# A hybrid mixer block: pacing the weight block sums and moving second-layer modulation products

## The reference

```python
mod = split(silu(c) @ ada_w[l] + ada_b[l], 6)             # for the latents
mod_c = split(silu(c_ctx) @ ada_w[l] + ada_b[l], 6)       # for the context
h = modulate(rmsnorm(x, norm1_w[l]), mod[0], mod[1])
p = split_cols(h @ w_in[l])                               # A, B, C, D and the gates
x = x + mod[2] * gated_merge([ya, yb, yg, yd], p[4], w_branch[l], w_o[l])
x = x + mod[5] * sqrelu_mlp(modulate(rmsnorm(x, norm2_w[l]), mod[3], mod[4]), mlp_w1[l], mlp_w2[l])
```

## Time and profile before

| | us |
|---|---|
| median of 3 runs | 2919.35 (2917.09 to 2925.95) |
| the profiled execution | 2913.71 |
| its span | 2911.9 |
| TensorE busy | 2754.0 |
| VectorE busy | 1728.8 |
| ScalarE busy | 1421.1 |
| GpSimd busy | 212.7 |
| mean granted clock of TensorE | 0.983 |

### The profile page before, as it was taken

One profiled execution on the slowest core, in us unless ns is written; L12 is line 12 of the kernel. 1 busy time (PEld: TensorE's weight loads), 2 busy tenths in 40 slices (PEclk: granted clock), 3 DMA queues, 4 the chain that ended last, 5 costly groups with the idle time before them and its releaser, 6 DMA issues.

```text
span 2911.9 us, 36847 instructions
## 1 busy us (share of the span) xinstructions
PE 2754.0 (95%) x14456; PEld 2299.8 (79%) x14456; DVE 1728.8 (59%) x2539; ACT 1421.1 (49%) x2335; POOL 212.7 (7%) x259
## 2 busy tenths in 40 slices
PE   6999999989989999899899999999999999999998
PEld 4888886778877778788899878777667776788887
DVE  4478843436645546887989552784547644654434
ACT  4644434435635545767676444444546635433222
POOL 0023311011001000000000000321000000000000
PEclk9999999999999999999999999999999999999999
DMA  6322167098269134345566232224021220423232
GB/s 243 116 66 71 64 208 179 15 273 213 77 193 263 41 131 152 125 152 162 185 204 210 82 107 68 88 95 146 11 92 62 88 66 20 165 82 100 94 98 90
DMA packets 100022, 356.46 MB, mean 122 GB/s; under 512 B 11216, under 2 KB 11472, under 8 KB 98640
## 3 DMA queue, kind: packets, MB, share of 16 engines
q1 hardware_dynamic: 79936, 248.19, 25.5%
q0 software_dynamic: 19920, 105.99, 13.2%
HBM read 327.91 MB, written 84.94 MB: 142 GB/s over the span
## 4 chain that ended last, share of the span: by engine, by line
PE 41%; DVE 6%; ACT 3%; issue 2%; DMA 1%; SPq 0%; DVEq 0%; ACTq 0%
PE slot L860 35%; PE slot L1394 4%; DVE wl L2185 1%; PE slot L1361 1%; DVE ada_prod L2844 1%; DMA raw<-w_merge_dram 1%; ACT b_high L2024 1%; ACT ada_prod L1965 1%; DMA raw<-w_dram 0%; ACT wh L1511 0%; DVE b_low L2774 0%; DVE X L2794 0%; ACT UR L2046 0%; DMA SS<-g_kept 0%; PE slot L1071 0%
## 5 line engine op out<-in xcount | busy, mean ns | idle before, releaser
L860 PE MATMUL slot<-Hh,wh 128*128 128x512 f32 (+1 forms) x1872 | 701.3, 376 | 29.5 <-issue 11.8
L860 PE MATMUL slot<-Hh,wl 128*128 128x512 f32 (+1 forms) x1872 | 665.7, 357 | 0.0
L860 PE MATMUL slot<-Hl,wh 128*128 128x512 f32 (+1 forms) x1872 | 664.8, 356 | 0.0
L2185 DVE TENSOR_TENSOR wl<-raw,wh 128x1024 fp32r<-128x1024 f32 (+1 forms) x374 | 430.4, 1151 | 278.8 <-ACT wh L1511 276.2
L1511 ACT ACTIVATE wh<-raw 128x1024 fp32r<-128x1024 f32 (+1 forms) x374 | 366.5, 981 | 390.7 <-PE slot L860 237.8
L860 PEld LDWEIGHTS slot<-Hh,wh 128*128 128x128 f32 x1872 | 357.4, 191 | 85.2 <-issue 25.3
L860 PEld LDWEIGHTS slot<-Hh,wl 128*128 128x128 f32 x1872 | 356.2, 191 | 51.4
L860 PEld LDWEIGHTS slot<-Hl,wh 128*128 128x128 f32 x1872 | 357.9, 192 | 48.0 <-issue 6.0
L1394 PE MATMUL slot<-b_high,wh 128*128 128x384 f32 x784 | 270.3, 345 | 33.1 <-DVE wl L2185 19.6
L1394 PE MATMUL slot<-b_low,wh 128*128 128x384 f32 x784 | 267.1, 341 | 0.0
L1394 PE MATMUL slot<-b_high,wl 128*128 128x384 f32 x784 | 266.8, 340 | 0.0
(11 more groups left out here) (314 smaller groups left out, 4843.5 us busy)
## 6 DMA issues: line engine op xcount, KB each, us to landing
raw<-w_dram SPq DMA_DIRECT2D x190, 512.0 KB, 3.6
raw<-w_gate_dram SPq DMA_DIRECT2D x64, 512.0 KB, 3.5
raw<-w_sums SPq DMA_DIRECT2D x56, 512.0 KB, 3.6
ada_g_raw<-ada_dram POOLq DMA_DIRECT2D x55, 512.0 KB, 4.3
raw<-w_merge_dram SPq DMA_DIRECT2D x64, 256.0 KB, 3.7
w_sums<-w_dram POOLq DMA_DIRECT2D x14, 1024.0 KB, 11.3
w_sums<-w_sums POOLq DMA_DIRECT2D x14, 1024.0 KB, 8.4
ada_g_raw<-ada_dram SPq DMA_DIRECT2D x25, 512.0 KB, 4.5
```

The source lines that it names most:

```text
L860: return pe.matmul(dst, lhsT, rhs, start=start, stop=stop)
L2185: dve.tensor_tensor(wl[to][:, 0:size, :], raw[p][:, 0:size, :], wh[to][:, 0:size, :].bitcast(f32), ALU.subtract).then_inc(low_done.sem, 1)
```

## The change

It changes the order of three kinds of work; what is computed stays the same.

- **Weight block sums.** Phases 0 and 1 go with attention A, 2 and 3 with B, 4 and 5 with D. Before each transfer GpSimd waits (`turn`) until TensorE has done one more attention tile's scores (24 tiles in A and D: one tile a transfer; 48 in B: three tiles a transfer). Phase 6 is issued during the blocks, one transfer after each of 8 modulation tiles.
- **Second layer's one-sided products** (tiles 48 to 79). They leave the blocks for the second layer itself: 10 in C's projection, 8 in D's, 11 in the output product (two each in its jobs 1, 2, 4 and 5), 3 in the first jobs of the MLP. `condition_rows` is issued in the second layer too, before D and before the output product. SyncE loads the tiles. The two-sided tiles 32 to 47 stay in the blocks, now at jobs 29 to 39, 57 to 67 and 85 to 91, every second one. `modulation_ready` for the second norm moves from the first to the last job of the second layer's output product.
- **Four gate tiles** (25 to 28) move from the blocks to the first layer's output product, whose jobs 1, 2, 4 and 5 have two tiles each; the last three stay at block jobs 5, 8 and 11. Of two tiles in a job, VectorE multiplies the first before the split and the second after it.

```diff
-        WEIGHT_SUMS = {"C": (), "A": (0, 1), "B": (2, 3, 4), "D": (5, 6)}
+        WEIGHT_SUMS = {"A": (0, 1), "B": (2, 3), "D": (4, 5)}
...
             if n == FIRST_FF + 1:
-                return 3
+                return 2
...
+        def ada_jobs(layer):
+
+            jobs = list(range(3, 13)) + list(range(FIRST_D[layer], FIRST_D[layer] + KT))
+            for n in range(KT - 1):
+                jobs += [FIRST_FF - KT + n] * (2 if n in (1, 2, 4, 5) else 1)
+            return jobs
+
+        ADA_JOBS = ada_jobs(0)
+        ADA_EARLY, ADA_SECOND, ADA_ALL = len(ADA_JOBS), N_GATE + ADA_BOTH, N_GATE + ADA_TILES
...
+        for t, n in enumerate(ada_jobs(1) + list(range(FIRST_FF + 1, FIRST_FF + 1 + N_GATE - ADA_EARLY))):
+            ADA_OF.setdefault(N_FIRST + n, []).append(ADA_SECOND + t)
+        ADA_AT = dict(zip((5, 8, 11), range(ADA_EARLY, N_GATE)))
+        ADA_AT |= dict(zip((29, 31, 33, 35, 37, 39, 57, 59, 61, 63, 65, 67, 85, 87, 89, 91), range(N_GATE, ADA_SECOND)))
...
-                if t == 0:
-                    sp.wait_ge(job_done.sem, 2)
+                if t in (0, ADA_SECOND):
+                    sp.wait_ge(job_done.sem, 2 if t == 0 else N_FIRST + 2)
...
+            def paced_sums(branch):
+
+                tiles, turns = len(attention_tiles(branch, 0)), 8 * len(WEIGHT_SUMS[branch])
+                for phase in WEIGHT_SUMS[branch]:
+                    weight_sums(phase, lambda: pool.wait_ge(scores_done.sem, w.next(scores_done, tiles // turns)))
...
-                    if layer == 0:
-                        for phase in WEIGHT_SUMS[b]:
-                            weight_sums(phase)
+                    if layer == 0 and b != "C":
+                        paced_sums(b)
...
-                        if layer == 0:
-                            condition_rows()
+                        condition_rows()
...
-                    modulation_tiles()
+                    tiles = iter(range(ADA_EARLY, ADA_SECOND))
+                    for _ in range(N_GATE - ADA_EARLY + 2):
+                        modulation_tile(next(tiles))
+                    weight_sums(BLOCK_PHASES - 1, lambda: modulation_tile(next(tiles)))
+                    for t in tiles:
+                        modulation_tile(t)
...
                 layer, n = place(jobs[0])
-                first_layer_product(layer, n)
+                tiles = ADA_OF.get(layer * N_FIRST + n, ())
+                for t in tiles[:1]:
+                    ada_product(t, ada_g_full[t % 2])
                 if n > 1 and n != EARLY + 1:
                     low(n + 1)
+                for t in tiles[1:]:
+                    ada_product(t, ada_g_full[t % 2])
...
-                        if wave:
-                            done(dve.tensor_copy(mod[:, ADA_FIRST:ADA_TILES, :], mod_next[:, ADA_FIRST:ADA_TILES, :]))
...
+                        if first and x == KT:
+                            dve.wait_ge(ada_summed.sem, ADA_ALL)
+                            add_bias(DEPTH - 1, MOD_GATE2, ADA_TILES)
```

More of the change, by code:

```diff
@@ L568, in home, with ada_column @@
             return n % 2
[L570 to L576, removed]
+        FIRST_D = [sum(N_PROJ[b] + n_gates[b] + KT for b in BRANCHES[:-1]) for n_gates in LATER_GATES]
+        def ada_jobs(layer):
[5 more added lines that the diff above has]
+        ADA_EARLY, ADA_SECOND, ADA_ALL = len(ADA_JOBS), N_GATE + ADA_BOTH, N_GATE + ADA_TILES
+        ADA_OF = {}
+        for t, n in enumerate(ADA_JOBS):
+            ADA_OF.setdefault(n, []).append(t)
+        for t, n in enumerate(ada_jobs(1) + list(range(FIRST_FF + 1, FIRST_FF + 1 + N_GATE - ADA_EARLY))):
+            ADA_OF.setdefault(N_FIRST + n, []).append(ADA_SECOND + t)
+        ADA_AT = dict(zip((5, 8, 11), range(ADA_EARLY, N_GATE)))
+        ADA_AT |= dict(zip((29, 31, 33, 35, 37, 39, 57, 59, 61, 63, 65, 67, 85, 87, 89, 91), range(N_GATE, ADA_SECOND)))
+        assert len(ADA_AT) == ADA_SECOND - ADA_EARLY
+        def ada_column(t, side):
+            if N_GATE <= t < ADA_SECOND:
+                return mod_next[:, t - N_GATE, side:side + 1]
+            t = t if t < N_GATE else t - ADA_SECOND
+            return mod[:, ADA_FIRST + t, side:side + 1]
         def ada_sides(t):
@@ L750, in _, with modulation_tile, weight_sums @@
             w = Counts(pool)
[L751 to L757, removed]
+            def modulation_tile(t):
+                pool.wait_ge(ada_read.sem, ADA_FIRST + t - 1)
+                pool.dma_start(ada_raw[t % 2][:, :, :], w_ada[ADA_FIRST + t]).then_inc(ada_full[t % 2].sem, 16)
+            def weight_sums(phase, turn):
                 def piece(ap):
@@ L837, in _ @@
                         tables(after, layer)
-                        if layer == 0 and after == BRANCHES[-1]:
+                        if after == BRANCHES[-1]:
                             condition_rows()
                     else:
-                        if layer == 0:
-                            condition_rows()
+                        condition_rows()
                         per = KT // X_PIECES
@@ L1946, in merged_high, with modulation_sums @@
                 act.activation(Mh[:, k, 0:nq], M[:, k, 0:nq], ACT.Copy).then_inc(m_high.sem, 1)
-            def first_layer_sum(layer, n):
-                if layer or n not in ADA_JOBS:
-                    return
-                t = ADA_JOBS.index(n)
-                act.wait_ge(ada_read.sem, w.next(ada_read, 1 + (0 if t else ADA_FIRST)))
-                for side in range(2):
-                    row = ada_prod[t % 2][:, side, :]
-                    ins = act.activation(row, row, ACT.Copy, accum_out=mod[:, ADA_FIRST + t, side:side + 1])
-                ins.then_inc(ada_summed.sem, 1)
+            def modulation_sums(layer, n):
+                for t in ADA_OF.get(layer * N_FIRST + n, ()):
+                    if t == 0:
+                        w.next(ada_read, ADA_FIRST)
+                    ada_sum(t)
             def ada_sum(t):
@@ L2935, in group @@
                             add_squares(x - KT - 1, nq)
+                        if first:
+                            for t in ADA_OF.get(N_FIRST + n + x, ()):
+                                ada_product(t, ada_g_full[t % 2])
+                        if first and x == KT:
+                            dve.wait_ge(ada_summed.sem, ADA_ALL)
+                            add_bias(DEPTH - 1, MOD_GATE2, ADA_TILES)
                         if over:
```

62 lines of the change are left out of this document (30 added, 32 removed).

## The result

Four executions after the change gave 2870.77 us (median; 2869.57 to 2872.84), four of the kernel before 2918.22 (2910.87 to 2925.95): a ratio of 0.9838, with a 95% interval of 0.9811 to 0.9864. That is 47 us less, against 38 forecast (2881 from 2919.35), and inside the range of 2852 to 2906.

What follows compares the result with a forecast made beforehand. TensorE was taken to bound the kernel wherever fed, leaving gaps and the slow clock behind them to win. Terms -32 -27.5 +7.5 +8.5 +6 = -37.5 us gave 2881 from 2919.35, range 2852 to 2906.

Steps and rivals of the forecast that it cites:

- part 2: First layer's block phases: fewer products and an on-time start remove gaps; gain 27.5 us (12 to 42).
- part 1: Starts of branches B and D: weight block sums moved into attention remove TensorE waits and slow clock; gain 32 us (20 to 38).
- part 3: First layer's output product: four more two-sided tiles make double jobs run over; loss 7.5 us (0 to 12).
- part 4: Second layer: one-sided products cost 0 in projections, 8.5 us in the output product; condition rows cost 6.
- The 3 us taken to stay at D: Start of branch D: table and condition rows still leave at B's merge, so 3 of 35.2 us stay.
- attention hides the transfers: Attention loads only a few weight tiles, each long ahead; a late last one in B costs some 3 us.
- The ring: Block phases: product, sums, high half, low halves and next product depend in turn, at 9.50, 8.73 and 11.21 us against 8.3.
- the last phase's sums: Beside phases 2 to 4: 8 transfers may each delay a load by 4.1 us against 3.3 slack; loss 2 (0 to 7).
- rival D: Second layer's jobs: product ahead of split and loads behind waiting loads cost something in each of 32 jobs; 2953 us, chance 0.04.
- Rival C: Moved transfers keep their price beside the blocks and at merges: 2924 us at worst, 2903 with slack; chance 0.07.
- Rival E: Sums chained too slowly in attention run into the merges; gain 32 falls to 10, 2903 us; chance 0.06.
- Rival A: Double tiles in both output products and the condition rows are hidden: 2859 us, chance 0.17.

Runs made afterwards that it cites:

- the run with one side a job: Changed kernel with each two-sided product of the blocks cut in two, one side's product and sum at one job, the other's at the next: 2865.34 us, 0.9814.

## Why the prediction was right, and where its terms were off

The sum, -37.5, came out at -44.1, and the mechanisms named are those found, with two steps of part 2 and one of part 1 wrong as told below. The sizes are off further than the sum: part 1 came out 6 us better than forecast, part 2 11.4 worse, part 3 1.9 better and part 4 8.4 better. That the misses of parts 2 and 4 nearly cancel is luck.

- **Part 1, -32 forecast, about -38 measured** (-15.5, -17.7 and -2.9 in the three stretches of B and D, and some of the first -3.7: A's projection had its own wait and slow clock from the first sums, for which I had no term; the rest of the 3.7 is 1.6 in the start of the program, before anything of the change). The upper third of my range. The 3 us taken to stay at D for table and condition rows didn't stay: no wait at D's start. The wait of D's merge that had been put on the condition rows was 3.0 us and is 1.7 with the same rows in the same place. Its one weak step is the one that this change happens not to need, that attention hides the transfers. It hides two phases in a branch, spread or not. It didn't hide three in B in any of the runs that had them, and in the one looked at the store of gate logits took 19.0 us.
- **Part 2, -27.5 forecast, -16.1 measured.** The ring is shown: with short products every phase from 2 on takes 58.2. Phases 1 and 3 fell to 60.4 and 60.3 (forecast 59 each), phase 0 by 7.9 (10). The term for a ring of two-sided products, 4.5 a phase, is 5.3. Two steps failed. First, phase 6: I let four products pass inside the slack at 0, and they cost 4.5. Second, the last phase's sums: I took one in three or four of them to hit a load (2 us of at most 6.4), and they cost 7.7, more than that bound. The bound took every late load at 7.7 us; in the changed kernel loads behind the accumulating transfers took up to 9.5, and in the run with one side a job all four hit. In the changed kernel two of them stand in phase 4, which takes 66.7 us with them and 63.5 without. The cost isn't a fixed one: with the same transfers in the blocks, four kernels take 445.3, 446.0, 445.0 and 441.3 us against 437.6 without, so 3.7 to 8.4.
- **Part 3, +7.5 forecast, +5.6 measured.** Double jobs 9.7 and 10.7 us (forecast 9.9 and 10.8), the single one 7.3 (7.3). Gaps of 1.0 and 2.1 us stand where 1.5 and 2.5 were forecast, the one of 0.3 is absent, and the norm's start is no later than before, where I had 1.0.
- **Part 4, +14.5 forecast, +6.1 measured.** The merges with the condition rows grew by 3.0 and 2.8 us (forecast 6 for both); at B the rows are shown to cost it, at D they aren't, since a kernel without rows there took 24.7 us. The output product's doubles cost 2.5 by the traces and 1.8 by undoing them, not 8.5: the term took gaps and a late norm of 4.8, a load term of 1.5 and the clock; the trace has new gaps of 0.9 and 1.2 us and none of the others. The one-sided products in C's and D's projections cost nothing, as forecast, and rival D with it is out.
- Rival C, that the transfers keep their price wherever they stand, is out: phase 0's eight transfers cost nothing in C, sixteen nothing in each attention, four plain copies nothing beside phase 2. They did slow loads and stores wherever they were looked at, as the Trainium skill's turn-taking rule has it; a forecast from the rule alone lacks the slack that hides the delay. Beside the blocks the rival is half right: the accumulating transfers cost 2 us each there, not 4.1. Rival E didn't come, since the sums ended before each merge. Rival A is half true: the second layer's doubles are nearly hidden, the first layer's aren't.

## What to carry to other kernels

A background transfer costs by what is waiting when it runs: put it where the engine that sets the pace has all its operands, and check every DMA of that stretch, stores that free a single buffer included, not only the weight loads. When a side job on a busy engine makes a ring of dependences longer than the period, cut it into pieces shorter than the slack before moving it elsewhere: nine or ten halves cost nothing in the phases where six whole products cost 5.3 us and four 4.5. And when extra work is put behind the split in a job, price it by the chain to the next job's end; that gave the double jobs' lengths to 0.2 us.

## What was unexpected of the hardware

- 1 MB DRAM-to-DRAM transfers that accumulate delayed weight loads more than plain copies of the same size: in the run with one side a job the loads behind the former took 7.0 to 9.5 us, those beside the latter at most 6.7, and the medians in the profile's page are 3.3 to 3.6. In the trace before (840:950) a plain copy is 16 pieces of 64 KB at 2.9 us, so each DMA engine is held for 2.9 us, and an accumulating transfer 256 pieces of 4 KB at 0.35 us, which holds it for 5.5. The kernel sets `max_dma_last_dim=4096` for the latter only; whether the adding or the small pieces cost the time, no run shows.
- A 384 KB store from SBUF took 19.0 us beside five DRAM-to-DRAM transfers of 1 MB, and 2.3 in the median of the page after the change, far more than its share by equal turns; its pieces were 3 KB and those of the plain copies 64 KB.
- With 384 KB stores and 512 KB loads at a fifth of the DMA engines' time (C's chain of levels), eight transfers had no cost at all.
